# A gated convolution layer: last tile finished in halves, last projection weights rounded earlier, output stage in turns, first roots spread by two wide products

## The reference

```python
hn = x * rsqrt(mean(x * x, -1) + 1e-6) * norm_g
a, b, gate = split(hn @ w_in, 3)                    # 1024 x 3072
u = a * sigmoid(b)
u = depthwise_causal_conv(u, conv_w, taps=31) + conv_b
u = (u - mean(u)) * rsqrt(var(u) + 1e-5) * ln_g + ln_b   # over the channels of a row
out = x + (silu(u) * silu(gate)) @ w_out            # 1024 x 1024
```

## Time and profile before

| | us |
|---|---|
| median of 3 runs | 354.79 (354.25 to 354.96) |
| the profiled execution | 354.75 |
| its span, first to last instruction | 352.9 |
| TensorE busy | 348.6 |
| VectorE busy | 325.0 |
| GpSimd busy | 267.2 |
| ScalarE busy | 229.7 |

### The profile page before, as it was taken

How to read it: one execution, slowest core, us unless ns; L and a number is a source line. 1 busy time by engine, 2 the same in 40 slices (tenths; PEclk the granted TensorE clock), 3 DMA queues, 4 the chain that set the end, 5 groups by cost and what they waited for, 6 DMA issues and landing times.

```text
span 352.9 us, 4764 instructions
## 1 busy us (share of the span) xinstructions
PE 348.6 (99%) x1564; PEld 289.6 (82%) x1564; DVE 325.0 (92%) x520; ACT 229.7 (65%) x330; POOL 267.2 (76%) x192
## 2 busy tenths in 40 slices
PE   8999999999999999999999999999999999999996
PEld 8888888888888888888888888888888888878786
DVE  5679799999999999989999998998799999999972
ACT  6889685567936870998669777975574872443400
POOL 0129999999999999789999999896695551359240
PEclk9999999999999999999999999999999999999999
DMA  8995011211410321404110410441733398047152
GB/s 276 414 412 206 27 61 59 79 42 59 119 61 8 93 81 59 119 2 119 59 60 3 119 59 12 109 119 60 238 121 120 119 390 326 0 139 237 44 207 90
DMA packets 30520, 43.51 MB, mean 123 GB/s; under 512 B 18336, under 2 KB 18848, under 8 KB 30496
## 3 DMA queue, kind: packets, MB, share of 16 engines
q1 hardware_dynamic: 30352, 43.21, 35.9%
q10 hardware_dynamic: 144, 0.00, 0.0%
HBM read 34.82 MB, written 4.19 MB: 111 GB/s over the span
## 4 chain that ended last, share of the span: by engine, by line
PE 92%; DVE 6%; issue 1%; DVEq 0%
PE mm L655 68%; PE acc L731 9%; PE mm L672 6%; PE mm L731 6%; DVE sgate L1280 2%; DVE x_lo L1260 2%; DVE nat L1292 2%; PE acc L777 1%; PE acc L712 1%; PE acc L722 1%; PE acc L649 0%; PE acc L643 0%; PE acc L645 0%; DVE ones L1083 0%; DVEq L1278 0%
## 5 line engine op out<-in xcount | busy, mean ns | idle before, releaser
L655 PE MATMUL mm<-x_hi,w_hi 128*128 128x512 f32 x352 | 137.4, 390 | 0.0
L655 PE MATMUL mm<-x_hi,w_lo 128*128 128x512 f32 x352 | 137.0, 389 | 0.0
L655 PE MATMUL mm<-x_lo,w_hi 128*128 128x512 f32 x352 | 136.9, 389 | 0.0
L1192 DVE SCALAR_TENSOR_TENSOR acc<-u,chan,acc 128x512 f32<-128x512 f32 x157 | 110.5, 748 | 0.1
L1514 POOL TENSOR_TENSOR pconv<-pconv,prod 128x512 f32<-128x512 f32 x60 | 77.0, 1306 | 1.3 <-ACT prod L886 1.3
L655 PEld LDWEIGHTS mm<-x_lo,w_hi 128*128 128x128 f32 x352 | 66.1, 188 | 13.7
L655 PEld LDWEIGHTS mm<-x_hi,w_lo 128*128 128x128 f32 x352 | 66.1, 188 | 13.7
L655 PEld LDWEIGHTS mm<-x_hi,w_hi 128*128 128x128 f32 x352 | 66.1, 188 | 13.6
L1192 DVE SCALAR_TENSOR_TENSOR acc<-u,w_sum,acc 128x512 f32<-128x512 f32 x90 | 67.3, 747 | 2.4 <-ACT acc L868 2.3
L886 ACT ACTIVATE prod<-u,chan 128x512 f32<-128x512 f32 x69 | 47.9, 716 | 19.8 <-POOL pconv L1514 18.4
L1458 POOL TENSOR_TENSOR w_lo<-raw,w_hi 128x1024 fp32r<-128x1024 f32 (+1 forms) x21 | 49.7, 2365 | 7.8 <-ACT w_hi L835 7.8
(11 more groups left out here) (111 smaller groups left out, 528.2 us busy)
## 6 DMA issues: line engine op xcount, KB each, us to landing
raw<-w_in SPq DMA_DIRECT2D x22, 512.0 KB, 3.3
nat<-x_t SPq DMA_DIRECT2D x16, 256.0 KB, 5.4
sgate<-x SPq DMA_DIRECT2D x8, 512.0 KB, 10.4
raw<-w_out SPq DMA_DIRECT2D x8, 512.0 KB, 3.2
nat<-x SPq DMA_DIRECT2D x8, 512.0 KB, 8.3
y<-nat SPq DMA_DIRECT2D x15, 256.0 KB, 2.1
raw_late<-w_out SPq DMA_DIRECT2D x4, 512.0 KB, 4.5
sig<-w_out SPq DMA_DIRECT2D x4, 512.0 KB, 4.1
```

The costliest lines, as they stand in the source:

```text
L655: ins = nc.tensor.matmul(bank(("unit", m, h)), w[:, m % 3, k, :], xx[:, k, half(h)], start=(k == 0 and i == 0), stop=(k == KC - 1 and i == 2))
L1192: ins = nc.vector.scalar_tensor_tensor(dst, chain_in(j, chain, k), tap(j, chain, k), chain_bank(j, chain), ALU.mult, ALU.add)
```

## The change

Five edits stand in one diff:

- `spread_rms(0)` takes the form of h = 1. GpSimd splits `rms` into `rms_hi` and `rms_lo` (four small instructions); ScalarE makes eight diagonals in `diags` instead of four in `sgate`; TensorE makes two products of 128x512, one step later (`SPREAD_AT`).
- `y_odd`, `less` and `y_even` of tile 7 are made for 256 columns at a time, and VectorE's `split_half` of a half follows directly behind its three.
- ScalarE's `split_w(23)` goes ahead of its two `split_half`.
- The spreads of the two means and of the first deviation go two steps k earlier.
- The low weights of b = 4 go from GpSimd to VectorE; GpSimd's low weights of b = 5 wait for VectorE's `split_v(5)`; VectorE adds the results of b = 2 and b = 4 in another order.

```diff
-SHARED += [("merge", 0), ("sum", 15), ("y_odd", 0), ("less", 0), ("y_even", 0)]
+SHARED += [("merge", 0), ("sum", 15)] + [(end, h) for h in range(2) for end in ("y_odd", "less", "y_even")]
-MEAN_SPREAD_AT = {(22, 1, 2): 0, (22, 1, 6): 1}
-RSTD_SPREAD_AT = {(22, 1, 4): 0, (23, 0, 0): 1}
+MEAN_SPREAD_AT = {(22, 1, 0): 0, (22, 1, 4): 1}
+RSTD_SPREAD_AT = {(22, 1, 2): 0, (23, 0, 0): 1}
-            18: (225, 225, 243), 19: (243, 243, 262), 20: (262, 262, 272), 21: (272, 272, 272),
+            18: (225, 225, 243), 19: (243, 243, 262), 20: (262, 262, 275), 21: (275, 275, 275),
-SPREAD_AT = {1: (0, 4), 0: (3, 0, 2)}
+SPREAD_AT = {1: (0, 4), 0: (3, 0, 3)}
...
-         ("lo", 4, 0), ("lo", 4, 1),
...
-W_BY_VECTOR = {("+11", 4, 0): 1, ("+11", 4, 1): 2, ("lo", 3, 0): 3, ("lo", 3, 1): 4}
+W_BY_VECTOR = {("+11", 4, 0): 1, ("+11", 4, 1): 2, ("lo", 3, 0): 3, ("lo", 3, 1): 4, ("lo", 4, 0): 5, ("lo", 4, 1): 6}
-W_PAUSES = {("22-12", 2, 0): CK, ("lo", 2, 0): 2 * CK, ("21-", 3, 0): 4 * CK, ("12-11", 5, 0): 5 * CK, ("lo", 6, 0): 7 * CK}
+W_PAUSES = {("22-12", 2, 0): CK, ("lo", 2, 0): 2 * CK, ("21-", 3, 0): 4 * CK, ("12-11", 5, 0): 5 * CK, ("lo", 5, 0): 6 * CK, ("lo", 6, 0): 7 * CK}
...
@@ TensorE: spread_rms(h)
-                    for i in range(TPH):
-                        pe.wait_ge(diag_ready, i + 1)
-                        ins = nc.tensor.matmul(rms_spread(0)[:, i * P:(i + 1) * P], ones[:], diag(i), start=True, stop=True)
+                pe.wait_ge(diag_hi_ready if h == 1 else first_hi_ready, TPH)
+                nc.tensor.matmul(spread, ones_r[:], diags[:, 0, :, :], start=True, stop=False)
+                pe.wait_ge(diag_lo_ready if h == 1 else first_lo_ready, TPH)
+                nc.tensor.matmul(spread, ones_r[:], diags[:, 1, :, :], start=False, stop=True).then_inc(rms_all_ready, 1)
@@ ScalarE: called with tiles 0 to 2, then with tile 3
+            def rms_diagonals(tiles):
+                act.wait_ge(ident_in, 16)
+                act.wait_ge(rms_all_ready, 1)
+                act.wait_ge(rms_ready, rms_count(tiles[-1]))
+                for t in tiles:
+                    nc.scalar.activation(diags[:, 0, t, :], ident[:], ACT.Copy,
+                                         scale=rms[:, t:t + 1]).then_inc(first_hi_ready, 1)
+                act.wait_ge(rms_lo_ready, 2 if TPH - 1 in tiles else 1)
+                for t in tiles:
+                    nc.scalar.activation(diags[:, 1, t, :], ident[:], ACT.Copy,
+                                         scale=rms_lo[:, t:t + 1]).then_inc(first_lo_ready, 1)
...
@@ ScalarE, unit 21
                 if m == NU - 3:
+                    split_w(m + 2)
                     for h in range(NH):
                         split_half(h)
-                    split_w(m + 2)
@@ VectorE
+                    for h in range(NH):
+                        if done == STEP[SHARED_TILE, "y_even", h]:
+                            split_half(h)
...
-            for h in range(NH):
-                split_half(h)
...
-            posts(2, (1,))
+            posts(2, (1, 2))
+            for i in range(2):
+                finish_wb_lo(4, i)
             for k in range(CK):
                 sum_v(5, k)
-            posts(2, (2, 3))
+            posts(2, (3,))
...
-            posts(4, (0, 1))
+            posts(4, (0,))
             for k in range(CK):
                 split_v(5, k)
+            posts(4, (1, 2))
...
-            posts(4, (2, 3))
+            posts(4, (3,))
@@ GpSimd: behind each of the two inverse_rms
+            def split_rms(tiles):
+                part = slice(tiles[0], tiles[-1] + 1)
+                n = 2 if TPH - 1 in tiles else 1
+                pool.wait_ge(rms_ready, rms_count(tiles[0]))
+                nc.gpsimd.tensor_scalar(rms_hi[:, part], rms[:, part], 1.0, None, ALU.mult).then_inc(rms_hi_ready, 1)
+                pool.wait_ge(rms_hi_ready, n)
+                nc.gpsimd.tensor_tensor(rms_lo[:, part], rms[:, part], rms_hi[:, part].bitcast(F32),
+                                        ALU.subtract).then_inc(rms_lo_ready, 1)
...
-                if op == ("lo", 4, 0):
-                    pool.wait_ge(vsum_ready, vsum_count(5, CK - 1))
```

More of the change, by code:

```diff
@@ L115, in gated_conv_layer @@
     STEP = {step: n + 1 for n, step in enumerate(STEPS)}
-    STEP_END = {j: STEP[j, "y_even", 0] for j in VECTOR_TILES}
+    STEP_END = {j: STEP[j, "y_even", int(j == SHARED_TILE)] for j in VECTOR_TILES}
     FIRSTS = [(j, chain) for j in VECTOR_TILES for chain in CHAINS]
@@ L162, in gated_conv_layer @@
         sig = sb("sig", [P, 2, HALF])
-        sb("gap_before_w", [P, 96])
+        rms_hi = sb("rms_hi", [P, TPH], F32R)
+        rms_lo = sb("rms_lo", [P, TPH])
+        sb("gap_before_w", [P, 80])
         first = ExitStack()
@@ L199, in gated_conv_layer @@
         ones_r_ready = sem("ones_r_ready")
-        diag_ready = sem("diag_ready")
+        first_hi_ready = sem("first_hi_ready")
+        first_lo_ready = sem("first_lo_ready")
+        rms_hi_ready = sem("rms_hi_ready")
+        rms_lo_ready = sem("rms_lo_ready")
         diag_hi_ready = sem("diag_hi_ready")
@@ L637, in spread_rms @@
             def spread_rms(h):
+                spread = rms_spread(h).rearrange("p (t q) -> p t q", t=TPH)
                 if h == 1:
[L640 removed]
                     pe.wait_ge(ones_r_ready, 1)
[L642 to L650 removed]
+                pe.wait_ge(diag_hi_ready if h == 1 else first_hi_ready, TPH)
+                nc.tensor.matmul(spread, ones_r[:], diags[:, 0, :, :], start=True, stop=False)
+                pe.wait_ge(diag_lo_ready if h == 1 else first_lo_ready, TPH)
+                nc.tensor.matmul(spread, ones_r[:], diags[:, 1, :, :], start=False, stop=True).then_inc(rms_all_ready, 1)
             def unit_terms(m, h, k):
@@ L989, in _ @@
             split_x(1, 2)
-            for t in range(TPH):
-                rms_diagonal(t)
+            rms_diagonals(range(TPH - 1))
+            rms_diagonals((TPH - 1,))
             split_x(1, 3)
@@ L1165, in step @@
                 j, chain, k = STEPS[n]
+                part = slice(Q * k, Q * (k + 1)) if j == SHARED_TILE else slice(0, HALF)
                 if chain == "less":
                     dve.wait_ge(steps_done, STEP[j, "sum", HT - 1])
-                    ins = nc.vector.tensor_tensor(y_part(j, 0), chain_bank(j, "sum"), odd_sum[:], ALU.subtract)
+                    ins = nc.vector.tensor_tensor(y_part(j, 0)[:, part], chain_bank(j, "sum")[:, part], odd_sum[:, part],
+                                                  ALU.subtract)
                 elif chain == "y_odd":
@@ L1173, in step @@
                         dve.wait_ge(xlo_pool, NH * KC)
-                    ins = nc.vector.tensor_tensor(y_part(j, 1), chain_bank(j, "before"), odd_sum[:], ALU.add)
+                    ins = nc.vector.tensor_tensor(y_part(j, 1)[:, part], chain_bank(j, "before")[:, part], odd_sum[:, part],
+                                                  ALU.add)
                 elif chain == "merge":
@@ L1180, in step @@
                 elif chain == "y_even":
-                    dve.wait_ge(steps_done, STEP[j, "less", 0])
-                    ins = nc.vector.tensor_tensor(y_part(j, 0)[:, 1:HALF], y_part(j, 0)[:, 1:HALF],
-                                                  chain_bank(j, "before")[:, 0:HALF - 1], ALU.subtract)
+                    dve.wait_ge(steps_done, STEP[j, "less", k])
+                    late = slice(max(part.start, 1), part.stop)
+                    ins = nc.vector.tensor_tensor(y_part(j, 0)[:, late], y_part(j, 0)[:, late],
+                                                  chain_bank(j, "before")[:, late.start - 1:late.stop - 1], ALU.subtract)
                 else:
@@ L1524, in _ @@
                 finish_x_lo(1, k)
-            inverse_rms(range(TPH - 1))
-            inverse_rms((TPH - 1,))
+            for tiles in (range(TPH - 1), (TPH - 1,)):
+                inverse_rms(tiles)
+                split_rms(tiles)
             for k in range(2, KC):
```

20 lines of the change are left out of this document (4 added, 16 removed), and 2 rows, old and new, of the table STEPS_BY.

## The result

The changed kernel takes 356.75 us (median of 20 executions, 355.29 to 358.36), the kernel before 354.72 beside it (20 executions, 354.25 to 355.28): a ratio of 1.0050, 95% interval 1.0039 to 1.0062. It is slower by 2.0 us where 0.6 was forecast, and the median lies outside the range.

A forecast was written before the change was run, and what follows sets the result against it. TensorE was taken as the bound, busy 348.6 of 352.9 us, with at most 1.0 us to win from waits. Terms -0.45 + 1.65 - 0.2 - 0.77 + 0.35 = +0.6 on 354.75 gave 355.3 us, range 353.8 to 356.1.

The forecast's parts named there:

- The wide products: First roots' spread on TensorE: two wide products take 0.45 us where four fp32 products cost 0.90; -0.45 us.
- its main sum on TensorE: Whole kernel, TensorE's work and pauses: -0.45 + 1.65 - 0.2 - 0.77 + 0.35 = +0.6 us, giving 355.3.
- its second one, on VectorE: Whole kernel: VectorE sets the last pause, so the change is its lateness (0.9 us) less 0.3 to 0.4.
- The lateness carried to tile 7: First x_lo to tile 7: GpSimd's full 1.2 us of lateness carries through, so tile 7's ends start at 244.6.
- Rival 1: Tile 7: GpSimd's lateness doesn't reach it (0.3 instead of 1.2), all behind comes 0.9 earlier; 354.4 us, chance 0.2.
- The held copy: End of tile 7: GpSimd's w_lo(23) holds VectorE's copy of half 0, due at 245.9, until 247.8.
- Rivals 2 and 3: At half 0's copy: 2, not held, lateness as forecast, 354.1 us, chance 0.1; 3, neither, mean in time, 353.3, chance 0.08.
- Rival 4: First roots: GpSimd's small low parts cost as a root (0.85 for three, 0.54 for one); 356.1 us, chance 0.14.
- The pause at the mean: First mean spread: means at 253.45, wanted at 251.9; TensorE pauses 1.55 us plus 0.1 for the restart, +1.65.
- the pause at 316: Output stage: split_v(4) comes 1.15 us earlier and TensorE's hesitation there goes, -0.2 us.
- that at k = 1: Output stage, b = 5: TensorE's old pause waiting for VectorE's split_v(5) goes, -0.77 us.
- a new one of 0.38 at k = 2: Output stage, b = 5: TensorE waits for GpSimd's second low weight, ready 329.8, wanted 329.5; about +0.35 us.

The follow-up runs named there:

- c3_no_roots: The changed kernel with only the edit of the first roots (spread_rms(0)) undone: 354.41 us, ratio 0.9993 to the kernel before.
- b1: The changed kernel with ScalarE's split_w(23) put back behind the two split_half: 356.78 us, ratio 1.0054 to the kernel before.
- b2: The kernel before with one number changed, the first spread of the means asked for six steps k earlier: 358.05 us, ratio 1.0071.
- b5: The kernel before with the two wide products, the four low diagonals made by VectorE, no new GpSimd instruction: 357.99 us, ratio 1.0089.
- the one of 388.86: One of six executions of the kernel before with the first-roots edit alone, at mean clock 0.85; that kernel's median 356.73 us, ratio 1.0062.

## Why the prediction was wrong

By its own steps, with 0.69 taken off the changed kernel's times:

- **The wide products** come out as costed: two starts 0.23 apart (36.50, 36.73), no pause there. GpSimd's small instructions too: 35.21 against 35.2. The term -0.45, though, bought nothing here: TensorE then stood 2.46 us waiting for the mean, and work saved ahead of a wait only lengthens it. That is read from the timeline; no run has the term alone (c3_no_roots, which has that work back and is 2.2 us faster, also takes the lateness away). The prediction named VectorE as the one that sets the last pause, and then made its main sum on TensorE; its second one, on VectorE, took centring 0.9 late, and it was 1.48.
- **The lateness carried to tile 7** is 0.99, not 1.2 (244.42, forecast 244.6). Rival 1 is out. What was missed is a second way to the same lateness: ScalarE's diagonals ahead of the x_hi that GpSimd reads next. "ScalarE is 1.2 us behind, which moves `copy_rms(0)` by 0.3 us only" looked at one of its readers. In the changed kernel the two coincide, so the number came out right, in part by luck.
- **The held copy**: right, 1.79 us, ended at 247.4 (forecast 247.8). Rivals 2 and 3 are out. Rival 4 too: the low parts took 0.20 and 0.19.
- **The pause at the mean: the term that was mis-sized.** +1.65 was forecast (1.55 and 0.1 for the restart), 2.46 came (2.53 with the restart). The transpose was given 2.76 us from its issue, from one row; here it took 3.68 (248.20 to 251.88), and over the series 2.7 to 2.8 or 3.4 to 3.9 for both halves together, 3.0 to 3.7 for a half alone (4.85 in b1). The means stood at 254.1, forecast 253.45, and were asked for at 251.8.
- **The step that was missing: what so long a pause does to the clock.** No term of the sum has a price for the products behind the pause. With 2.4 to 2.7 us of pause 21 of 38 executions (changed kernel, b1, b2, b5) show the lower clock; with up to 1.04 in the profile none did but the one of 388.86. b2_pause shows that the pause alone is enough. The nine executions at the full clock have a median of 355.61, which the range holds; the eleven others bring the median of all to 356.75, out of it.
- **The output stage**: as forecast, the pause at 316 gone, that at k = 1 gone, a new one of 0.38 at k = 2 (forecast 0.35). But that is no net gain of 0.6: measured by the rest, the edit is worth 0.4, and alone 0.1 in the medians (354.51 against 354.58), which is within the interval.

Made on VectorE, the sum is: tile 7 late 0.99, halves and transposes 0.49 (12.05 instead of 11.56 from tile 7's ends to centring), rest -0.37: +1.11, as the two spans say (321.87 against 320.76 from the mark); the medians at the full clock differ by 0.89 (355.61 against 354.72). The rest of the 2.0 is the clock.
